# Stick-breaking heads scored in pairs with fp32 suffix products, and differential matrices combined before their transposition

## The chip, the cores and the metric

The kernel runs on one core of a Trainium2 chip as one program. The metric is the device time of one execution in microseconds (us). The engines are TensorE (PE, with its weight loads as PEld), VectorE (DVE), ScalarE (ACT), GpSimd (POOL) and SyncE (SP), which here issues the loads of the weights. They run side by side and meet through semaphores.

## What is computed

256 tokens of width 1024 pass through two layers of a first block and two layers of a second block, all in fp32. The first block (mLSTM, block-sparse and compressed attention, feed-forward) is not touched. A layer of the second block is:

```python
h = rms_norm(x, g_pre)
qa, ka, va, ga, qs, ks, vs, gs, qf, kf, vf, gf, ff = split(h @ w_in)   # 12 x 512 columns, and 8
ya = diff_attention(rope(qa), rope(ka), va, lam, lambda_init, subln) * silu(ga)
yb = stick_breaking_attention(qs, ks, vs) * silu(gs)
yc = forgetting_attention(qf, kf, vf, cumsum(log_sigmoid(ff + f_bias))) * silu(gf)
x = x + rms_norm(concat([ya, yb, yc]) @ w_out, g_post)
```

Differential attention has 4 heads of two softmax matrices each, over 64 features, and a value of width 128:

```python
p = softmax(where(allowed, s, -inf))        # for both matrices of a head
w = p[:, :, 0] - lam * p[:, :, 1]
o = w @ v                                   # then rms_norm(o, sub_gain) * (1 - lambda_init)
```

Stick-breaking attention has 8 heads of 64 features:

```python
log_keep = where(strict, log_sigmoid(-z), 0.0)
log_rest = cumsum(log_keep, reverse=True) - log_keep
a = where(strict, exp(log_sigmoid(z) + log_rest), 0.0)
o = a @ v
```

## The kernel before

**Units.** Nearly all work is the weight products. A unit is 512 KB of weights, 256 rows by 512 columns or 128 by 1024. SP loads it to one of four buffers `raw`; ACT copies it to `w_hi` in fp32r (L1193); DVE, for some units GpSimd, takes the remainder `w_lo` = `raw` - `w_hi` (L1561); PE then makes three products of parts, hi x hi, hi x lo and lo x hi (L754 to L756). ACT and DVE prepare the unit three ahead of the one at which PE stands (`AHEAD = 3`). A buffer of w_hi is free again when PE has finished the unit four before, which is what `released` waits for.

**Order.** Each layer has one list of steps, written out by hand; every engine walks through the same list in the same order and does its own part of each step. In the second block, `side2(p)` puts the attention steps behind unit p of the layer (12 projections of four units, p = 0 to 47, then the output units). `GROUPS`, `LAGS` or `V_LAG` and the numbers in `side2` say at which p a stage of a head stands. On each engine all steps wait in this order: an instruction that waits for a semaphore holds everything behind it on its engine.

**Differential heads**, 8 matrices h, from p = 12 on, one and a half units apart. S: scores of h and h+1 issued in turn, with the first on partitions 0 to 63 and the second on 64 to 127, to PSUM banks 4 and 5 (`score_pair`, L869); DVE adds the mask, takes the row maxima and writes to one of three buffers `probs` (L1639 to L1645). E: ACT's exponentials with their row sums (L1231, L1233). T: three transpositions on PE (L897) and ACT's copy to `probsT` (L1237). V: three products with the values (L904 to L906). After both matrices of a head, `epilogue_diff` on DVE takes the reciprocals of the row sums, scales the two results, adds them and sums their squares (L1959 to L1967). After the last one GpSimd applies norm, gain and gate (L1522 to L1530).

**Stick-breaking heads**, h = 0 to 7, from p = 26 on, one and a half units apart, with keys on the partitions. Z: two fp32 score products of 256 and 128 columns and two bf16 products that add the mask (L1120 to L1123), then on ACT abs, exp and log of 384 columns (L1422 to L1424) to `softp`, two buffers. K, one unit later: DVE adds max(z, 0) from PSUM (L2062) and splits the sum to `keep_hi` and `keep_lo` in fp32r (L2066, L2067). R, three units after Z: six fp32r products with the constant matrices `suffix` (L1130 to L1132) subtract the suffix sums from the scores, in the same PSUM bank; ACT's exp to `probs` (L1426). V, four units after Z: three products with the values (L1143 to L1145); `gated` multiplies by the gates.

**Forgetting heads** follow from p = 41 on with the same stages as the differential ones (S with two more products at L878).

Of the kernel before, what the change touches and what calls it, by code (L numbers as in the profile page):

```python
# [99 lines left out]
def hybrid_blocks(nc, x, w_in, b_if, conv_qk, m_norm, moba_qk_norm, nsa_q_norm, nsa_k_norm, cmp_pe,  # L100
# [78 lines left out]
    def head_steps(name, h, stage, groups_of):  # L179


        if stage == "S" and h % 2 == 0:
            for c in range(2):
                use((*name, "S", h + c), 4 + c)
        elif stage == "T":
            use((*name, "T", h), 6)
        elif stage == "V":
            g, r = divmod(h, groups_of)
            if r == 0:
                use((*name, "O", g), 7)  # L190
            if r == groups_of - 1:
                done((*name, "O", g))
        step(*name, stage, h)

    def stick_steps(l, h, stage):


        if stage == "Z":
            use(("stick", l, "Z", h), 4 + h % 3)
        elif stage == "R":  # L200
            use(("stick", l, "R", h), 4 + h % 3)
# [169 lines left out]
    for l in range(L):  # L371
# [75 lines left out]
    with ExitStack() as ctx:  # L447
# [52 lines left out]
        suffix = sb("suffix", [P, 2, P], F32R)  # L500
# [33 lines left out]
        row_sum, row_inv = few(2, 4, NT), few(4, NT)  # L534
        kc_s = few(4)
# [35 lines left out]
        keep_hi, keep_lo = exact("keep_hi", vecs_at, 0, 2, 384), exact("keep_lo", vecs_at, 768, 2, 384)  # L571
# [40 lines left out]
        diff_mixed = sem("diff_mixed")  # L612
        mix_ready = sem("mix_ready")
        u_hi_ready, u_ready = sem("u_hi_ready"), sem("u_ready")
        keep_ready = sem("keep_ready")
# [113 lines left out]
        def _(pe):  # L729
# [152 lines left out]

            def head_stage(kind, l, stage, h):
                name = (kind, l)
                if stage == "E":
# [6 lines left out]
                elif stage == "T":  # L892

                    pe.wait_ge(exp_ready, nth_head(kind, l, h))
# [4 lines left out]
                else:  # L899
                    g, r = divmod(h, GROUPS[kind])  # L900
                    drained(pe, (*name, "T", h))
# [5 lines left out]
                    if r == GROUPS[kind] - 1:  # L907
# [176 lines left out]
            for l in range(L):  # L1084
                for s in timeline[1][l]:
# [28 lines left out]
                    elif kind == "stick" and s[2] == "Z":  # L1114
                        h = s[3]
                        head_inputs(kind, l, "Z", h)
                        b = HD * (h % 2)
                        q, k = featT[b:b + HD, h // 2, :], featT[b:b + HD, 4 + h // 2, :]
                        ps = open_bank(("stick", l, "Z", h))
                        pe.matmul(ps[:, 0:T], k[:, 0:P], q, start=True, stop=False, skip_group_check=True)  # L1120
                        pe.matmul(ps[:, T:T + P], k[:, P:T], q[:, P:T], start=False, stop=False, skip_group_check=True)
                        pe.matmul(ps[:, 0:P], ident_b, strict_b, start=False, stop=False, skip_group_check=True)
                        close(pe.matmul(ps[:, T:T + P], ident_b, strict_b, start=False, stop=False, skip_group_check=True), s)  # L1123
# [44 lines left out]
        def _(act):  # L1168
# [201 lines left out]
            for l in range(L):  # L1370
                for s in timeline[1][l]:
# [744 lines left out]
```

## Time and profile before

| | |
|---|---|
| Median of 3 runs | 1177.3 us (1176.02 to 1179.41) |
| Profiled execution | 1181.94 us, span 1180.1 us, granted clock 0.974 |
| PE busy | 1131.2 us (96%) |
| PEld busy | 989.7 us (84%) |
| DVE busy | 741.5 us (63%) |
| ACT busy | 627.6 us (53%) |
| POOL busy | 111.7 us (9%) |
| Chain that ended last | PE 77%, DVE 13%, ACT 6%, issue 3% |

The span runs from the first to the last instruction; what is missing to the execution's own time lies around it. Layer 0 of the second block is at about 721 to 941 us of the span, layer 1 from there to the end. Busy time of PE counts pipelined products, whose printed durations overlap; the distance of two starts is what one takes. One fp32 product of the program stands as two records in the timeline.

### The profile page before, as it was taken

The page shows a single profiled execution, that of the slowest core. Times are in us where ns is not written, and L with a number is a line of the kernel's source. Part 1 is how long each engine was busy: PE and PEld are TensorE (multiplying, and loading weights), DVE is VectorE, ACT ScalarE, POOL GpSimd, SP SyncE. Part 2 cuts the span into 40 slices and gives each one's busy share as a digit, 9 for nine tenths or more (in the row PEclk, how much of TensorE's full clock was granted, in tenths as well). Part 3 has the DMA queues.
Part 4 walks back from the last instruction along what each step waited for, and adds up shares of the span by engine and source line. Part 5 has one row for each costly group of instructions (what it writes and reads, how often), then busy time and mean ns, then how long its engine had stood idle before and what let it go on. Part 6 is the DMA issues. An engine that isn't in the chain of part 4 may idle for free.

```text
span 1180.1 us, 17617 instructions
## 1 busy us (share of the span) xinstructions
PE 1131.2 (96%) x6888; PEld 989.7 (84%) x6888; DVE 741.5 (63%) x1275; ACT 627.6 (53%) x989; POOL 111.7 (9%) x99
## 2 busy tenths in 40 slices
PE   8899989999999899989999999999999989999997
PEld 6788779889988788769899887798988767989885
DVE  4786657555556876667555556667555566775555
ACT  4544655544545535746444545565657446656572
POOL 0324010000000324110000000003000000030000
PEclk8988999999999988999999999999999989999999
DMA  8625235555555425235555555444443445444431
GB/s 295 187 77 165 101 107 195 179 191 185 180 195 168 153 77 170 93 112 190 185 187 188 180 189 186 159 147 139 125 143 107 143 151 161 146 126 132 143 123 56
DMA packets 88959, 181.16 MB, mean 154 GB/s; under 512 B 8669, under 2 KB 19805, under 8 KB 88877
## 3 DMA queue, kind: packets, MB, share of 16 engines
q1 hardware_dynamic: 87437, 175.78, 45.9%
q10 hardware_dynamic: 1440, 4.26, 1.0%
q8 instruction: 55, 0.90, 0.3%
q14 instruction: 27, 0.22, 0.1%
HBM read 178.97 MB, written 1.05 MB: 153 GB/s over the span
## 4 chain that ended last, share of the span: by engine, by line
PE 77%; DVE 13%; ACT 6%; issue 3%; DMA 1%; POOL 1%; DVEq 0%; POOLq 0%; SPq 0%; ACTq 0%
PE bank L754 22%; PE bank L756 21%; PE bank L755 21%; DVE w_lo L1561 2%; PE bank L831 2%; ACT w_hi L1193 2%; PE bank L992 2%; PE bank L869 1%; PE bank L897 1%; DVE vecs L1570 1%; PE bank L1120 1%; DVE xn L1847 1%; PE bank L905 1%; PE bank L906 1%; PE bank L904 1%
## 5 line engine op out<-in xcount | busy, mean ns | idle before, releaser
L1561 DVE TENSOR_TENSOR w_lo<-raw,w_hi 128x1024 fp32r<-128x1024 f32 x296 | 366.3, 1241 | 297.6 <-ACT w_hi L1193 293.9
L1193 ACT ACTIVATE w_hi<-raw 128x1024 fp32r<-128x1024 f32 (+1 forms) x320 | 335.1, 1051 | 240.0 <-PE bank L756 205.7
L754 PE MATMUL bank<-h_hi,w_hi 128*128 128x256 f32 x896 | 262.7, 293 | 3.6 <-DVE w_lo L1561 2.1
L755 PE MATMUL bank<-h_lo,w_hi 128*128 128x256 f32 x896 | 257.5, 287 | 0.0
L756 PE MATMUL bank<-h_hi,w_lo 128*128 128x256 f32 x896 | 257.3, 287 | 0.0
L754 PE MATMUL bank<-w_hi,h_hi 128*128 128x512 f32 (+1 forms) x448 | 183.1, 409 | 5.8 <-DVE h_lo L1580 5.3
L754 PEld LDWEIGHTS bank<-h_hi,w_hi 128*128 128x128 f32 x896 | 176.1, 197 | 8.5 <-DVE w_lo L1561 3.4
L755 PEld LDWEIGHTS bank<-h_lo,w_hi 128*128 128x128 f32 x896 | 176.2, 197 | 0.5
L755 PE MATMUL bank<-w_lo,h_hi 128*128 128x512 f32 (+1 forms) x448 | 176.6, 394 | 0.0
L756 PE MATMUL bank<-w_hi,h_lo 128*128 128x512 f32 (+1 forms) x448 | 176.5, 394 | 0.0
L756 PEld LDWEIGHTS bank<-h_hi,w_lo 128*128 128x128 f32 x896 | 175.9, 196 | 0.0
L754 PEld LDWEIGHTS bank<-w_hi,h_hi 128*128 128x128 f32 x448 | 85.9, 192 | 23.9 <-DVE w_lo L1561 6.0
L754 PE MATMUL bank<-w_hi,u_hi 128*128 128x512 f32 x256 | 101.3, 396 | 0.0
L756 PEld LDWEIGHTS bank<-w_hi,h_lo 128*128 128x128 f32 x448 | 86.1, 192 | 17.8
L756 PE MATMUL bank<-w_hi,u_lo 128*128 128x512 f32 x256 | 101.0, 395 | 0.0
L755 PE MATMUL bank<-w_lo,u_hi 128*128 128x512 f32 x256 | 101.0, 394 | 0.0
L755 PEld LDWEIGHTS bank<-w_lo,h_hi 128*128 128x128 f32 x448 | 86.2, 192 | 14.8
L1455 POOL TENSOR_TENSOR w_lo<-raw,w_hi 128x1024 fp32r<-128x1024 f32 (+1 forms) x24 | 57.9, 2416 | 104.5 <-ACT w_hi L1193 104.4
L1237 ACT ACTIVATE probsT<-bank 128x384 f32<-128x384 f32 x56 | 27.4, 489 | 70.6 <-PE bank L897 70.1
L754 PE MATMUL bank<-w_hi,mixT_hi 128*128 128x512 f32 x128 | 54.1, 422 | 3.9 <-DVE mixT_lo L1580 3.9
L756 PEld LDWEIGHTS bank<-w_hi,u_lo 128*128 128x128 f32 x256 | 48.2, 188 | 11.3
L754 PEld LDWEIGHTS bank<-w_hi,u_hi 128*128 128x128 f32 x256 | 48.3, 189 | 10.4
(295 smaller groups left out, 1502.2 us busy)
## 6 DMA issues: line engine op xcount, KB each, us to landing
raw<-in_w_in SPq DMA_DIRECT2D x144, 512.0 KB, 3.8
raw<-in_w_ff SPq DMA_DIRECT2D x128, 512.0 KB, 4.0
raw<-in_w_out SPq DMA_DIRECT2D x40, 512.0 KB, 3.2
raw<-in_cmp_w SPq DMA_DIRECT2D x8, 512.0 KB, 4.5
raw<-in_w_in SPq DMA_DIRECT2D x8, 404.0 KB, 3.8
x_sb<-in_x SPq DMA_DIRECT2D x2, 512.0 KB, 7.4
gain<-in_norm_ffn ACTq DMA_DIRECT2D x2, 512.0 KB, 6.5
gain<-in_pre_norm ACTq DMA_DIRECT2D x2, 512.0 KB, 5.0
```

Of the source, the lines that this page charges most:

```text
L754: pe.matmul(out_ap, s_hi, m_hi, start=start, stop=False, **kw)
L755: pe.matmul(out_ap, s_hi, m_lo, start=False, stop=False, **kw)
L756: return pe.matmul(out_ap, s_lo, m_hi, start=False, stop=stop, **kw)
L831: mm = pe.transpose(ps[:, n * P:(n + 1) * P], src[:, i, k * P:(k + 1) * P], ident)
L869: mm = pe.matmul(ps[c][:, lo:lo + cols], q[:, i * P:(i + 1) * P], k[:, 0:cols], start=i == 0, stop=i == 1 and last == "scores", skip_group ...
L897: mm = pe.transpose(ps[:, b * P:(b + 1) * P], probs[:, h % 3, b * P:(b + 1) * P], ident)
L904: pe.matmul(ps[:, lo:lo + width], probsT[:, h % 3, 0:P], value(0), start=True, stop=True)
L992: mm = pe.matmul(ps[:, 16 * v:16 * v + NC_CMP], w[:, a, :], blocksT[:, v, 8 * half + a, :], start=(half == 0 and a == 0), stop=(half == 1 ...
L1193: act.activation(slot(w_hi, u), slot(raw, u), ACT.Copy).then_inc(hi_ready, 1)
L1237: free(act.activation(probsT[:, h % 3, :], ps[:, 0:384], ACT.Copy), (*name, "T", h))
L1455: pool.tensor_tensor(slot(w_lo, u), slot(raw, u), slot(w_hi, u).bitcast(F32), ALU.subtract)\
L1561: dve.tensor_tensor(slot(w_lo, u), slot(raw, u), slot(w_hi, u).bitcast(F32), ALU.subtract)\
```

## The change

- Differential heads: a new stage C between E and T. DVE computes `first + second * factor` for the exponentials of the two matrices of a head, with factor = -lam * (sum of first) / (sum of second) per row, in place in `first` (`combine_diff`). T and V run for even h only. `epilogue_diff` reads one result of 256 columns and multiplies it by the reciprocal of the first sum. T stands one unit later than before, and GpSimd's norm follows `V` of h = 6 at p = 25, before h = 7 at p = 26.
- Stick-breaking heads: Z of h and h+1 in one step every three units (`stick_pair`), products of the two heads in turn, to banks 4 and 5. K of both one unit later, R of both two units later, V of h three and of h+1 four units later. K keeps its first operation only; R makes three fp32 products from `softp` with the constants themselves. `keep_hi`, `keep_lo`, `suffix` and the semaphore `keep_ready` go.

```diff
         elif stage == "V" and name[0] == "diff":
+            use((*name, "O", h // 2), 7)
+            done((*name, "O", h // 2))
...
-        V_LAG = {"diff": 4, "fox": 3}
+        LAGS = {"diff": (("V", 4), ("T", 3), ("C", 2), ("E", 1), ("S", 0)), "fox": (("V", 3), ("T", 2), ("E", 1), ("S", 0))}
...
-                for stage, lag in (("V", V_LAG[name[0]]), ("T", 2), ("E", 1), ("S", 0)):
-                    for h in range(8):
+                for stage, lag in LAGS[name[0]]:
+                    for h in range(0, 8, 2 if name[0] == "diff" and stage in ("V", "T", "C") else 1):
...
-            for stage, lag in (("V", 4), ("R", 3), ("K", 1), ("Z", 0)):
+            for stage, lag in (("V", 3), ("R", 2), ("K", 1), ("Z", 0)):
                 for h in range(8):
-                    if int(26 + 1.5 * h) + lag == p:
+                    late = h % 2 if stage == "V" else 0
+                    if 26 + 3 * (h // 2) + lag + late == p:
                         stick_steps(l, h, stage)
...
+            def stick_pair(l, h):
...
+                for lo, i in ((0, 0), (T, 1)):
+                    for c in range(2):
+                        b = HD * c
+                        q, k = featT[b:b + HD, h // 2, i * P:T], featT[b:b + HD, 4 + h // 2, i * P:(i + 1) * P]
+                        pe.matmul(ps[c][:, lo:lo + T - i * P], k, q, start=i == 0, stop=False, skip_group_check=True)
+                for lo in (0, T):
+                    for c in range(2):
+                        mm = pe.matmul(ps[c][:, lo:lo + P], ident_b, strict_b, start=False, stop=False, skip_group_check=True)
+                        if lo:
+                            close(mm, keys[c])
...
-                    pe.wait_ge(exp_ready, nth_head(kind, l, h))
+                    if kind == "diff":
+                        pe.wait_ge(diff_weights, 4 * l + h // 2 + 1)
+                    else:
+                        pe.wait_ge(exp_ready, nth_head(kind, l, h))
...
-                        pe.wait_ge(keep_ready, 8 * l + h + 1)
                         ps = open_bank(("stick", l, "R", h))
-                        for kp in (keep_hi[:, h % 2, :], keep_lo[:, h % 2, :]):
-                            pe.matmul(ps[:, 0:T], suffix[:, 0, :], kp[:, 0:T], start=False, stop=False, skip_group_check=True)
-                            pe.matmul(ps[:, P:T], suffix[:, 1, :], kp[:, T:T + P], start=False, stop=False, skip_group_check=True)
-                            mm = pe.matmul(ps[:, T:T + P], suffix[:, 0, :], kp[:, T:T + P], start=False, stop=False,
-                                           skip_group_check=True)
-                        close(mm, s)
+                        keep = softp[:, h % 2, :]
+                        after, every = const[:, C_RTRI:C_RTRI + P], const[:, C_NONES:C_NONES + P]
+                        pe.matmul(ps[:, 0:T], after, keep[:, 0:T], start=False, stop=False, skip_group_check=True)
+                        pe.matmul(ps[:, T:T + P], after, keep[:, T:T + P], start=False, stop=False, skip_group_check=True)
+                        close(pe.matmul(ps[:, P:T], every, keep[:, T:T + P], start=False, stop=False, skip_group_check=True), s)
...
-                        if h >= 2:
-
-                            act.wait_ge(keep_ready, 8 * l + h - 1)
...
-                    elif s == ("diff", l, "V", 7):
+                    elif s == ("diff", l, "V", 6):
...
-                        link(dve.tensor_copy(suffix[:, 0, :], const[:, C_RTRI:C_RTRI + P]))
-                        link(dve.tensor_copy(suffix[:, 1, :], const[:, C_NONES:C_NONES + P]))
...
+                def combine_diff(g):
+
+                    first, second = probs[:, (2 * g) % 3, :], probs[:, (2 * g + 1) % 3, :]
+                    inv, factor = row_inv[:, 0:2, :], row_inv[:, 2, :]
+                    dve.wait_ge(exp_ready, nth_head("diff", l, 2 * g + 1))
+                    link(dve.reciprocal(inv, row_sum[:, g % 2, 0:2, :]))
+                    link(dve.scalar_tensor_tensor(factor, inv[:, 1, :], lam[:, 3:4], row_sum[:, g % 2, 0, :], ALU.mult, ALU.mult))
+                    link(dve.tensor_copy(first_inv[:, g % 2, :], inv[:, 0, :]))
+                    link(dve.scalar_tensor_tensor(first[:, 0:P], second[:, 0:P], factor[:, 0:1], first[:, 0:P], ALU.mult, ALU.add))
+                    dve.scalar_tensor_tensor(first[:, P:3 * P], second[:, P:3 * P], factor[:, 1:2], first[:, P:3 * P],
+                                             ALU.mult, ALU.add).then_inc(diff_weights, 1)
...
-                    ov = src(name)[:, :].rearrange("p (c i d) -> p c i d", c=2, i=NT)
-                    inv = row_inv[:, 0:2, :]
-                    link(dve.reciprocal(inv, row_sum[:, g % 2, 0:2, :]))
-                    link(dve.tensor_scalar(inv[:, 1, :], inv[:, 1, :], lam[:, 3:4], None, ALU.mult))
-                    t = o_tmp[:, :].rearrange("p (c i d) -> p c i d", c=2, i=NT)
-                    free(dve.tensor_tensor(t, ov, inv.unsqueeze(3).broadcast_to([P, 2, NT, P]), ALU.mult), name)
-                    tt(y_diff[:, :, g, :], t[:, 0], t[:, 1], ALU.add)
+                    ov = src(name)[:, 0:2 * P].rearrange("p (i d) -> p i d", i=NT)
+                    free(dve.tensor_tensor(y_diff[:, :, g, :], ov, first_inv[:, g % 2, :].unsqueeze(2).broadcast_to([P, NT, P]),
+                                           ALU.mult), name)
...
-                        if h >= 2:
-
-                            filled(dve, ("stick", l, "R", h - 2))
-                        link(dve.tensor_copy(keep_hi[:, h % 2, :], softp[:, h % 2, :]))
-                        dve.tensor_tensor(keep_lo[:, h % 2, :], softp[:, h % 2, :], keep_hi[:, h % 2, :].bitcast(F32),
-                                          ALU.subtract).then_inc(keep_ready, 1)
```

## Rows read from the trace of the kernel before

**Rows 1.** Stretches: bounds, busy us (instructions) per engine, granted clock, DMA share, GB/s.
```profile
820.00:860.00 40.00, 40.00 (x290) 37.03 (x288) 25.35 (x32) 25.42 (x39) 5.84 (x3) 1.00 0.39 125
```

**Rows 2.** Waits of PE, 740 to 926 us: total, times, longest.
```profile
PE bank L897 <- ACT probs L1233: 0.7, 1, 0.7
PE bank L754 <- DVE w_lo L1561: 0.3, 1, 0.3
```

**Rows 3.** Timeline of PE, V and T of differential heads: start us, duration, instruction.
```profile
778.27 0.38 PE L904 MATMUL bank<-arena,probsT 128*128 128x128 f32 x2
...
778.94 0.49 PE L897 MATMUL bank<-const,probs 128*128 128x128 f32 x3
779.18 0.36 PE L754 MATMUL bank<-h_hi,w_hi 128*128 128x256 f32 x1
779.39 0.28 PE L755 MATMUL bank<-h_lo,w_hi 128*128 128x256 f32 x1
779.50 0.28 PE L756 MATMUL bank<-h_hi,w_lo 128*128 128x256 f32 x1
```

**Rows 4.** Timeline of PE, the first two T of a layer.
```profile
767.40 0.49 PE L897 MATMUL bank<-const,probs 128*128 128x128 f32 x3
767.65 0.48 PE L754 MATMUL bank<-w_hi,h_hi 128*128 128x512 f32 x1
...
770.49 0.49 PE L897 MATMUL bank<-const,probs 128*128 128x128 f32 x3
```

**Rows 5.** Timeline of PE, last differential V and first stick scores.
```profile
811.83 0.39 PE L904 MATMUL bank<-arena,probsT 128*128 128x128 f32 x2
...
812.59 0.70 PE L1120 MATMUL bank<-arena 64*128 64x256 f32 x2
...
813.44 0.23 PE L1122 MATMUL bank<-masks 128*128 128x128 bf16 x1
...
813.54 0.48 PE L754 MATMUL bank<-w_hi,h_hi 128*128 128x512 f32 x1
```

**Rows 6.** Timeline of PE, the scores of a differential pair.
```profile
760.96 0.93 PE L869 MATMUL bank<-vecs 64*128 64x128 f32 x8
761.82 0.50 PE L754 MATMUL bank<-w_hi,h_hi 128*128 128x512 f32 x1
```

**Rows 7.** Timeline of PE, suffix products of the first and the last head.
```profile
822.93 0.28 PE L1130 MATMUL bank<-keep_hi,suffix 128*128 128x256 f32 x1
...
823.65 0.70 PE L1120 MATMUL bank<-arena 64*128 64x256 f32 x2
...
1099.08 0.36 PE L1130 MATMUL bank<-keep_hi,suffix 128*128 128x256 f32 x1
...
1099.79 0.44 PE L754 MATMUL bank<-w_hi,h_hi 128*128 128x512 f32 x1
```

**Rows 8.** Timeline of DVE behind the first stick scores.
```profile
816.35 1.22 DVE L1561 TENSOR_TENSOR w_lo<-raw,w_hi 128x1024 fp32r<-128x1024 f32 x1 [0.91 <-ACT w_hi L1193]
817.50 0.55 DVE L2062 SCALAR_TENSOR_TENSOR vecs<-bank,vecs 128x384 f32<-128x384 f32 x1
...
820.26 2.17 DVE L1561 TENSOR_TENSOR w_lo<-raw,w_hi 128x1024 fp32r<-128x1024 f32 x1
```

**Rows 9.** Timeline of DVE, a remainder ahead of the first T.
```profile
767.13 1.23 DVE L1561 TENSOR_TENSOR w_lo<-raw,w_hi 128x1024 fp32r<-128x1024 f32 x1 [1.17 <-ACT w_hi L1193]
```

**Rows 10.** Timeline of PE, fp32 products of full height in the first block.
```profile
504.00 0.65 PE L1040 MATMUL bank<-xn 128*128 128x256 f32 x2
504.49 0.39 PE L1041 MATMUL bank<-xn 128*128 128x128 f32 x2
```

**Rows 11.** Timeline of ACT behind the first stick scores.
```profile
813.76 0.49 ACT L1422 ACTIVATE vecs<-bank 128x384 f32<-128x384 f32 x1 [4.02 <-PE bank L1123]
...
815.28 1.04 ACT L1193 ACTIVATE w_hi<-raw 128x1024 fp32r<-128x1024 f32 x1
```

**Rows 12.** Timeline of GpSimd, two products of the differential norm.
```profile
820.05 3.53 POOL L1529 TENSOR_TENSOR xn<-xn,sub_gain 128x512 f32<-128x512 f32 x2
```

More of the change, by code:

```diff
@@ L186, in head_steps @@
             use((*name, "T", h), 6)
+        elif stage == "V" and name[0] == "diff":
+            use((*name, "O", h // 2), 7)
+            done((*name, "O", h // 2))
         elif stage == "V":
@@ L195, in stick_steps @@
     def stick_steps(l, h, stage):
-        if stage == "Z":
-            use(("stick", l, "Z", h), 4 + h % 3)
+        if stage == "Z" and h % 2 == 0:
+            for c in range(2):
+                use(("stick", l, "Z", h + c), 4 + c)
         elif stage == "R":
-            use(("stick", l, "R", h), 4 + h % 3)
+            use(("stick", l, "R", h), 4 + h % 2)
         elif stage == "V":
@@ L499, in hybrid_blocks @@
         rows = sb("rows", [8, 3, T])
-        suffix = sb("suffix", [P, 2, P], F32R)
         row_stack = sb("row_stack", [STACK, T], F32R)
@@ L534, in hybrid_blocks @@
         row_sum, row_inv = few(2, 4, NT), few(4, NT)
+        first_inv = few(2, NT)
         kc_s = few(4)
@@ L570, in hybrid_blocks @@
         softp = vecs[:, 3072 + 2048:3072 + 2048 + 768].rearrange("p (b t) -> p b t", b=2)
-        keep_hi, keep_lo = exact("keep_hi", vecs_at, 0, 2, 384), exact("keep_lo", vecs_at, 768, 2, 384)
         post_gain = vecs[:, 1536:1536 + D]
@@ L611, in hybrid_blocks @@
         h_ms_ready, h_rstd_ready = sem("h_ms_ready"), sem("h_rstd_ready")
-        diff_mixed = sem("diff_mixed")
+        diff_weights, diff_mixed = sem("diff_weights"), sem("diff_mixed")
         mix_ready = sem("mix_ready")
         u_hi_ready, u_ready = sem("u_hi_ready"), sem("u_ready")
-        keep_ready = sem("keep_ready")
         copied, sel_ready = sem("copied"), sem("sel_ready")
@@ L881, in score_pair @@
                                 close(mm, pair[c][0])
+            def stick_pair(l, h):
+                head_inputs("stick", l, "Z", h)
+                keys = [("stick", l, "Z", h + c) for c in range(2)]
+                ps = [open_bank(key) for key in keys]
+                for lo, i in ((0, 0), (T, 1)):
[4 more added lines that the diff above has]
+                for lo in (0, T):
+                    for c in range(2):
+                        mm = pe.matmul(ps[c][:, lo:lo + P], ident_b, strict_b, start=False, stop=False, skip_group_check=True)
+                        if lo:
+                            close(mm, keys[c])
             def head_stage(kind, l, stage, h):
                 name = (kind, l)
-                if stage == "E":
+                if stage in ("E", "C"):
                     return
@@ L900, in head_stage @@
                     g, r = divmod(h, GROUPS[kind])
+                    last = kind == "diff" or r == GROUPS[kind] - 1
                     drained(pe, (*name, "T", h))
@@ L906, in head_stage @@
                     mm = pe.matmul(ps[:, lo + width:lo + 2 * width], probsT[:, h % 3, 2 * P:3 * P], value(1), start=False, stop=True)
-                    if r == GROUPS[kind] - 1:
+                    if last:
                         close(mm, (*name, "O", g))
@@ L1114, in _ @@
                     elif kind == "stick" and s[2] == "Z":
[L1115 to L1123, printed above, removed]
+                        if s[3] % 2 == 0:
+                            stick_pair(l, s[3])
                     elif kind == "stick" and s[2] == "R":
                         h = s[3]
-                        pe.wait_ge(keep_ready, 8 * l + h + 1)
                         ps = open_bank(("stick", l, "R", h))
-                        for kp in (keep_hi[:, h % 2, :], keep_lo[:, h % 2, :]):
-                            pe.matmul(ps[:, 0:T], suffix[:, 0, :], kp[:, 0:T], start=False, stop=False, skip_group_check=True)
-                            pe.matmul(ps[:, P:T], suffix[:, 1, :], kp[:, T:T + P], start=False, stop=False, skip_group_check=True)
-                            mm = pe.matmul(ps[:, T:T + P], suffix[:, 0, :], kp[:, T:T + P], start=False, stop=False,
-                                           skip_group_check=True)
-                        close(mm, s)
+                        keep = softp[:, h % 2, :]
[3 more added lines that the diff above has]
+                        close(pe.matmul(ps[:, P:T], every, keep[:, T:T + P], start=False, stop=False, skip_group_check=True), s)
                     elif kind == "stick" and s[2] == "V":
@@ L2049, in _ @@
                             row_max((kind, l), s[3], C_CHUNK if kind == "diff" else C_CAUSAL)
+                        elif s[2] == "C":
+                            combine_diff(s[3] // 2)
+                        elif s[2] == "V" and kind == "diff":
+                            epilogue_diff(s[3] // 2)
                         elif s[2] == "V" and s[3] % GROUPS[kind] == GROUPS[kind] - 1:
                             g = s[3] // GROUPS[kind]
-                            if kind == "diff":
-                                epilogue_diff(g)
-                            else:
-                                gated(("fox", l, "O", g), 2, g, row_sum[:, g % 2])
+                            gated(("fox", l, "O", g), 2, g, row_sum[:, g % 2])
                     elif kind == "stick" and s[2] == "K":
```

## The prediction

> **What bounds the kernel now.** I first read the table of stretches. Between 820 and 860 us, in the part of the second block where the stick-breaking heads run, TensorE (PE) is busy 40.00 of 40 us at a granted clock of 1.00, while VectorE (DVE) and ScalarE (ACT) are busy 25.35 and 25.42 us [rows 1]. Next the list of waits, for PE alone over layer 0 of the second block: the largest entry is 0.7 us, and it belongs to the forgetting heads, which the change leaves alone [rows 2]. So PE is the bound, with no slack to give away, and the other engines only matter where a new wait makes PE stand still. Then the timeline of PE, where I take the distance from one start to the next, since the printed durations overlap. A half matmul of a weight product follows the last one by 0.11 to 0.12 us, but the first behind a head's step takes 0.21 us [rows 3]; each interruption of the weight stream thus costs about 0.09 us beside its own work. Last the timelines of ACT and DVE, for the chains that will feed PE.
>
> **Differential heads.** Before, every one of the 8 matrices of a layer has its own transposition (T) and product with V (V). Now DVE folds the second of a pair into the first, and T and V run for even h alone: four of each go per layer. A V and the T behind it run from 778.27 to 779.18, 0.67 + 0.24 = 0.91 us [rows 3]. In the places of a layer this gives: at step 14 a T alone, 0.25 us [rows 4]; at steps 17, 20 and 23 a V and a T, 3 x 0.91 = 2.73 us; at step 26 a V of 0.76 us [rows 5], of which I keep 0.09 us, since the scores behind it must still break into the stream. Sum 3.65 us. At steps 14, 17, 20 and 23 nothing is left between two units, which saves 4 x 0.09 = 0.36 us. That is 4.0 us per layer, **8.0 us** for both. ACT loses four copies per layer, which is off the path and worth nothing.
>
> What comes in is DVE's combination (step C): a reciprocal, two operations on two or four elements, and two scalar-tensor-tensors of 128 and 256 columns. No such operation from SBUF alone is in the trace; the nearest row is the 384-column one of the stick heads, 0.55 us [rows 8]. Five times that, 2.75 us, is the upper end; 0.55 us for all the columns together, with small ones at nothing, the lower. I take 1.5 us, because three of the five are tiny. The epilogue loses two operations of about the same work, so DVE's load stays; with 25 of 40 us it has room [rows 1]. Is T late? C(0) stands in DVE's queue behind the remainder (w_lo) of a unit that ends at 767.13 + 1.23 = 768.36 [rows 9]; plus 1.5 gives 769.9. T(0) now comes where T(1) was, 770.49 [rows 4], less the 0.34 us saved at step 14: 770.15. It fits by 0.3 us, so I price the wait at nothing. Behind C wait the next remainder, needed three units later, and the row maxima of the next pair. At the upper end of C, T would be late by 1.0 us, 8 us over the eight pairs.
>
> **Scores of the stick heads.** One head takes 0.85 us for its two fp32 products of 64 rows and 0.10 us for the two mask products: 812.59 to 813.54 [rows 5]. Sixteen are 15.2 us. The new step issues two heads in turn, on partitions 0 to 63 and 64 to 127. The scores of a differential pair are built so already: they hold the same 384 columns for each of two heads and take 0.86 us for both [rows 6], as much as one stick head alone. Add the masks, four instead of two: 0.10 to 0.35 us (what two take, and a whole stream of four as far apart as weight halves [rows 3]); I take 0.24. A pair costs 1.1 us, eight 8.8 us. Six of these now follow a V, where breaking in costs 0.09 us that an R step hid before: 0.5 us. Saving 15.2 - 9.3 = **5.9 us**. If the two heads did not overlap, it would be 2 x 0.95 = 1.9 us a pair and nothing saved.
>
> **Suffix sums.** Now six fp32r products per head, 0.72 us for the first [rows 7], 0.71 for the last; the sixteen read the same way lie between 0.62 and 0.81 and add up to 11.8 us. After: three fp32 products of 256, 128 and 128 columns. An fp32 product of 256 columns with full height takes 0.49 us including its entry [rows 10], so 0.40 without; one of 128 columns takes 0.67 / 3 = 0.22 us [rows 3]. That is 0.84 to 0.93; I take 0.88, 14.1 us in all: **+2.3 us**. Fewer instructions, then, but more PE time. A boundary less per layer in the stick part (-0.2 us for both).
>
> PE's own work thus changes by -8.0 - 5.9 + 2.3 - 0.2 = **-11.8 us**.
>
> **The new wait.** Before, R of a head came three units after its Z; now R of both heads comes two units after. In between lies: ACT's three operations per head, 815.28 - 813.76 = 1.52 us each [rows 11], for two heads; the next w_hi on ACT; its w_lo on DVE; and then the K of DVE. For one head K(0) began 817.50 and lasted 0.55, so it ended 4.51 us after the scores (813.54) [rows 5, 8]. With a second head on ACT ahead of the w_hi: 6.03 us. PE meanwhile has two units, 2 x 2.84 = 5.68 us (767.65 to 770.49 is one [rows 4]), and in the pairs 2 to 4 of a layer a V between them, 0.67 us more. So those three just fit, and the first pair of a layer waits 0.35 us. But GpSimd's norm of the differential heads runs beside it, 3.53 us for its two products [rows 12], and the w_lo that met it took 2.17 instead of 1.22 us [rows 8]. I expect it to meet this w_lo too: GpSimd starts one unit earlier, 4 us before what the row shows, but has further products behind these: +0.95 us on the chain. I take 1.2 us per layer, **+2.4 us**, with ends of 0 and 2.1 per layer. Behind the waiting R on PE stand the weight products; ACT and DVE run on meanwhile.
>
> How long DVE is held is where a rule of the Trainium skill weighs in (SBUF — State Buffer, section Who interferes with whom): a DVE instruction with two SBUF inputs and a GpSimd instruction reading SBUF exclude one another, and the second to start stands still until the first ends. The row agrees in kind, 2.17 us against 1.22. By the rule the K, with one input in PSUM, would not be held, but a w_lo that just missed could stand a whole GpSimd product; then the sum would come out about 1.8 us higher for both layers.
>
> The removed conversions of K (L2066, L2067) and of the suffix matrices (L1716, L1717) lie on DVE, which PE doesn't wait for here [rows 2]; I price them at nothing. No DMA is issued or moved.
>
> **Sum.** -11.8 + 2.4 = -9.4 us. The profiled execution took 1181.94 us (span 1180.1 and 1.8 around it), so 1172.5 of its kind. Its time lies 4.6 us above the median of 1177.3, which becomes 1167.9: **1168 us**.
>
> **Rivals.** (a) No stall: DVE's chain keeps up as it does now, and the whole 11.8 us shows, perhaps 1 more by cheaper masks: 1165. For it: only 0.35 us is missing without GpSimd. Against: the 2.17 us. (b) Slower: the chain of Z, ACT, w_hi, w_lo and K is late at every pair, because K falls behind one more remainder. A remainder comes once per unit, in step with the buffers that PE frees, so K would come one unit, 2.84 us [rows 4], after the time reckoned above: 3.2 us late at the first pair of a layer and 2.5 at the other three, 21.4 us in all, 1.9 more where GpSimd runs: 1177.3 - 11.8 + 23.3 = 1188.8. It decides from 11.8 / 8 = 1.5 us per pair on. For it: a margin of nearly nothing in three of four pairs, and a chain through four queued pieces of two engines. Against: the order of the queues, as the rows after 813.54 show it, has only one w_lo in front of K [rows 8]. (c) The two stick heads don't overlap, because their products begin with 256 columns and have masks behind: the 5.9 us go, 1173.8. Against: the differential pair of the same size takes 0.86 us. (d) The combination does not arrive in time for T at most pairs, 0.5 us each: 4 us back, 1172.
>
> **Chances.** Forecast as it stands 0.60; (a) 0.20; (c) 0.06; (d) 0.08; (b), or a half of it, 0.06. A change under 0.3%, 3.5 us, can't be told from none in this kernel. Forecast, (a), nearly all of (d) and half of (c) are faster: 0.91; same 0.05; slower 0.04. Range: down to (a) with the low ends of masks and R, 1163.5; up past the upper end of the two waits and (d), 1173.
>
> **What would show it.** Right: T and V of the differential heads half as many; a pair of stick scores about 1.1 us; R of two heads about 1.75 us in two equal parts; a gap on PE ahead of R of heads 0 and 1 in each layer, released by the K of DVE, and none ahead of the other R; GpSimd's products beside that w_lo. Wrong: gaps ahead of every R or T; two stick heads one behind the other; a granted clock below 1.00 in 740 to 920; an R over 1.0 us.

## The result, and the profile after

The changed kernel took 1162.56 us (median of 4 runs, 1160.23 to 1166.32) against 1177.47 (4 runs, 1176.02 to 1179.41): 14.9 us less. The ratio given with its 95% interval is 0.9864 (0.9839 to 0.9889), a little below the quotient of the two medians, 0.9873. The kernel is faster, and by more than the forecast 9.4 us: it ended 0.9 us below the range. Timed twice more, the same kernel gave ratios of 0.9928 and 0.9902 (below). All its 19 runs together have a mean of 1166.1 us (standard deviation 3.7), the 70 runs of the kernel before 1176.3 (3.0): 10.1 us less. The first timing was favourable to the change.

The page of the changed kernel, its span, busy time by engine, and the granted clock in 40 equal slices of the span, in tenths of full speed:

```profile
span 1159.3 us, 17421 instructions
...
PE 1109.0 (96%) x6816; PEld 967.6 (83%) x6816; DVE 722.1 (62%) x1257; ACT 622.8 (54%) x981; POOL 115.5 (10%) x99
...
PEclk9999999999999998999999999999999989999999
```

The profiled executions, 1181.94 and 1161.15 us, differ by 20.8. To see where, take two steps that the change doesn't touch: the last turned features before the second block, and the same of its layer 1. Timeline of PE, first before, then after:

```profile
721.53 0.66 PE L831 MATMUL bank<-const,xn 128*128 128x128 f32 x4 [0.47 <-DVE xn L1593]
...
941.30 0.66 PE L831 MATMUL bank<-const,xn 128*128 128x128 f32 x4 [1.09 <-DVE xn L1593]
```

```profile
711.20 0.66 PE L834 MATMUL bank<-const,xn 128*128 128x128 f32 x4 [0.48 <-DVE xn L1604]
...
926.01 0.66 PE L834 MATMUL bank<-const,xn 128*128 128x128 f32 x4 [1.10 <-DVE xn L1604]
```

Up to 721.53 and 711.20 both kernels run the first block, the same code but for two small casts: 10.3 us of the difference lie there. Layer 0 of the second block took 219.77 and 214.81, -5.0; layer 1 up to the last turned mix 216.17 and 210.65, -5.5; of this 0.2 lies in the piece ahead of the differential heads, which the change doesn't touch and which took 46.1 to 47.3 us in the profiles of either kernel. In what follows I cut the second block into stretches between such steps of PE. "Diff" runs from the turned features of the heads (756.39 us in the trace of before) to the first stick scores (812.59), "stick" from there to the first scores of the forgetting heads. All in us, each from one profile:

| kernel | block one | diff, layers 0 and 1 | stick, layers 0 and 1 |
|---|---|---|---|
| before | 721.53 | 56.20, 56.43 | 61.55, 61.55 |
| changed | 711.20 | 52.52, 52.39 | 60.30, 60.30 |

The rest of the second block, forgetting heads and output, is equal within 0.01 us in layer 0 (67.16 and 67.17).

**Differential heads after**, which answer to [rows 3]: V is followed by the weight stream, and the T behind it is gone.

```profile
764.14 0.38 PE L927 MATMUL bank<-arena,probsT 128*128 128x128 f32 x2
...
764.73 0.36 PE L757 MATMUL bank<-h_hi,w_hi 128*128 128x256 f32 x1
764.92 0.28 PE L758 MATMUL bank<-h_lo,w_hi 128*128 128x256 f32 x1
```

The new step C on DVE, behind the remainder that answers to [rows 9], and the T that waits for it, in the timelines of DVE and of PE:

```profile
757.10 1.23 DVE L1572 TENSOR_TENSOR w_lo<-raw,w_hi 128x1024 fp32r<-128x1024 f32 x1 [1.17 <-ACT w_hi L1207]
758.24 0.17 DVE L1968 RECIPROCAL small<-small 128x4 f32<-128x4 f32 x1
...
759.30 0.48 DVE L1972 SCALAR_TENSOR_TENSOR probs<-probs,small 128x256 f32<-128x256 f32 x1
```

```profile
759.84 0.55 PE L919 MATMUL bank<-const,probs 128*128 128x128 f32 x3
```

C takes 758.24 to 759.78, 1.54 us, and T starts 0.06 us after it. At this T and at the last one of each layer the margin was all used: there the weight load of T waits for C (three times in the second block, 1.1 us together, 0.4 at most). On PE little of it shows. The last T of layer 0 starts 0.37 us after the product ahead of it, where 0.23 is usual, and the next product 0.30 us after T for 0.25 before, so about 0.2 us is lost; at the other five T, C had ended 0.68 to 0.90 us before.

**Stick scores after** ([rows 5]): two heads in 0.85 us, four masks in 0.21 (a pair takes 1.06 us).

```profile
798.54 0.92 PE L895 MATMUL bank<-arena 64*128 64x256 f32 x8
799.39 0.40 PE L898 MATMUL bank<-masks 128*128 128x128 bf16 x4
799.60 0.48 PE L757 MATMUL bank<-w_hi,h_hi 128*128 128x512 f32 x1
```

**R of the first pair** ([rows 7]), with the one wait that is new; both heads take 1.78 us here, 1.67 to 1.78 elsewhere. Then DVE and GpSimd beside it ([rows 8, 12]), with the two GpSimd products of L1540 in rows of their own:

```profile
805.69 0.70 PE L1146 MATMUL bank<-vecs,const 128*128 128x256 f32 x2 [0.38 <-DVE vecs L2080]
806.23 0.38 PE L1147 MATMUL bank<-vecs,const 128*128 128x128 f32 x2
806.45 0.39 PE L1148 MATMUL bank<-vecs,const 128*128 128x128 f32 x2
806.67 0.60 PE L1146 MATMUL bank<-vecs,const 128*128 128x256 f32 x2
...
807.47 0.48 PE L757 MATMUL bank<-w_hi,h_hi 128*128 128x512 f32 x1
```

```profile
803.86 1.31 DVE L1572 TENSOR_TENSOR w_lo<-raw,w_hi 128x1024 fp32r<-128x1024 f32 x1 [5.27 <-ACT w_hi L1207]
805.09 1.14 DVE L2080 SCALAR_TENSOR_TENSOR vecs<-bank,vecs 128x384 f32<-128x384 f32 x2
806.31 1.22 DVE L1572 TENSOR_TENSOR w_lo<-raw,w_hi 128x1024 fp32r<-128x1024 f32 x1
```

```profile
802.79 1.30 POOL L1540 TENSOR_TENSOR xn<-xn,sub_gain 128x512 f32<-128x512 f32 x1
804.16 2.14 POOL L1540 TENSOR_TENSOR xn<-xn,sub_gain 128x512 f32<-128x512 f32 x1
806.38 3.42 POOL L1541 TENSOR_TENSOR mix<-xn,arena 128x1024 f32<-128x1024 f32 x1
```

The w_lo that should have been held took 1.31 us. It did meet GpSimd, but 0.23 us before the end of a product (802.79 + 1.30 = 804.09, where w_lo had started at 803.86). From then on GpSimd's products were the longer ones: the second of L1540 took 2.14 us for 1.30, and L1541, which began 0.07 us behind the next w_lo, took 3.42 us; in the trace of before the same product, L1530, took 2.39. The w_lo of before that took 2.17 us (820.26, [rows 8]) had started 0.21 us into such a product, the first of the two in [rows 12]:

```profile
820.05 1.30 POOL L1529 TENSOR_TENSOR xn<-xn,sub_gain 128x512 f32<-128x512 f32 x1
```

### The profile page after: what moved, and what is told of

Read it like the earlier page. It is cut to its first block, busy times and chain, and to the rows that moved or that the text cites. A ratio compares the mean times of both kernels' runs of the same rounds, so it can differ in the third digit from the quotient of the medians.

```text
span 1159.3 us, 17421 instructions
## 1 busy us (share of the span) xinstructions
PE 1109.0 (96%) x6816; PEld 967.6 (83%) x6816; DVE 722.1 (62%) x1257; ACT 622.8 (54%) x981; POOL 115.5 (10%) x99
## 4 chain that ended last, share of the span: by engine, by line
PE 75%; DVE 13%; ACT 6%; issue 3%; POOL 1%; DMA 1%; DVEq 0%; POOLq 0%; SPq 0%; ACTq 0%
PE bank L757 22%; PE bank L759 21%; PE bank L758 21%; DVE w_lo L1572 2%; ACT w_hi L1207 2%; PE bank L834 2%; PE bank L872 1%; PE bank L919 1%; DVE vecs L1581 1%; DVE xn L1856 1%; PE bank L1015 1%; PE bank L1146 1%; DMA raw<-in_w_in 1%; PE bank L929 1%; PE bank L928 1%
## 5 line engine op out<-in xcount | busy, mean ns | idle before, releaser
L757 PE MATMUL bank<-h_hi,w_hi 128*128 128x256 f32 x896 | 259.9, 290 | 4.5 <-DVE w_lo L1572 2.1
L757 PEld LDWEIGHTS bank<-h_hi,w_hi 128*128 128x128 f32 x896 | 173.6, 194 | 9.7 <-DVE w_lo L1572 3.1
L758 PEld LDWEIGHTS bank<-h_lo,w_hi 128*128 128x128 f32 x896 | 173.8, 194 | 0.5
L759 PEld LDWEIGHTS bank<-h_hi,w_lo 128*128 128x128 f32 x896 | 173.5, 194 | 0.0
L758 PEld LDWEIGHTS bank<-w_lo,h_hi 128*128 128x128 f32 x448 | 86.0, 192 | 14.9
L758 PEld LDWEIGHTS bank<-w_lo,u_hi 128*128 128x128 f32 x256 | 48.2, 188 | 10.4
```

Of the source, the lines that this page charges most:

```text
L757: pe.matmul(out_ap, s_hi, m_hi, start=start, stop=False, **kw)
L758: pe.matmul(out_ap, s_hi, m_lo, start=False, stop=False, **kw)
L759: return pe.matmul(out_ap, s_lo, m_hi, start=False, stop=stop, **kw)
```

## The experiments

**Is the first block part of the change?** The theory, A in what follows: the change is worth 10.5 us, all in the second block, and the rest of the 14.9 is the first block's own scatter. The rival, B: the change shortens the first block as well, since two casts are gone from it. First the kernel before, unchanged, once more.

> The unchanged kernel once more. The second block takes 219.8 us for layer 0 (from the first products of its first transpositions, 721.5, to those of layer 1, 941.3) and 216.2 us for layer 1 up to the last transpositions of the mix (1157.5). Theory A (the change is worth 10.5 us, all of it in the second block; the rest of the 14.9 us lies in the first block, whose time moves with the granted clock from execution to execution): the second block again takes 219.8 and 216.2 us within 0.5, and the first block, 721.5 us in the profile of before, comes out some us shorter this time, 712 to 721, with a higher mean clock than 0.974. Theory B (the first block of this kernel is always about 721 us, and the change shortened it): 720 to 722 again.

1177.27 us (12 runs, 1171.05 to 1181.48), ratio 0.9999 (0.9976 to 1.0021). Block one 719.04, diff 56.61 and 56.21, stick 61.55 and 61.54. The stretches of the second block repeat to a few tenths, the first block moved by 2.5 us. Layer 1 as a whole took 215.4 us, 0.8 less than in the first profile, where I had allowed 0.5; 0.6 of that lies in the piece ahead of the differential heads. Now the changed kernel, unchanged.

> The changed kernel once more. Theory A: the second block takes 214.8 and 210.7 us again, the first block anything between 711 and 721 us, and against the kernel before the ratio of medians lies at 1 - 10.5/1177 = 0.991, with chance excursions of some us. Theory B: first block 711 us again, ratio 0.986 to 0.988 as in the first timing.

1167.88 us (9 runs, 1161.64 to 1172.69), ratio 0.9928 (0.9901 to 0.9955). Block one took **721.65** us, as in the first profile of the kernel before; diff 52.64 and 52.41, stick 60.30 and 60.33. So the changed kernel has the long first block too: the rival falls. What differs is the granted clock. Over the five profiles of the two kernels (one of them is shown at the end of the experiments) the mean granted clock of the execution and the length of block one go together: 0.973 and 721.65 us, 0.974 and 721.53, 0.976 and 719.04, 0.983 and 715.91, 0.984 and 711.20. Table of stretches (bounds, length, busy us of PE, PEld, DVE, ACT, POOL, granted clock, DMA share, GB/s) of before, of the first profile of the changed kernel, and of this one:

```profile
80.00:90.00 10.00, 10.00 (x64) 10.00 (x64) 7.25 (x16) 2.66 (x5) 0.00 (x0) 0.67 0.51 150
...
440.00:450.00 10.00, 10.00 (x65) 9.50 (x64) 1.46 (x9) 4.15 (x5) 4.72 (x2) 0.70 0.46 155
```

```profile
80.00:90.00 10.00, 10.00 (x78) 10.00 (x77) 6.28 (x13) 3.66 (x6) 1.05 (x1) 0.83 0.68 205
...
440.00:450.00 10.00, 10.00 (x78) 9.17 (x77) 7.46 (x23) 5.81 (x15) 3.77 (x3) 1.00 0.61 211
```

```profile
80.00:90.00 10.00, 10.00 (x64) 10.00 (x64) 7.23 (x16) 2.61 (x5) 0.00 (x0) 0.67 0.51 149
...
440.00:450.00 10.00, 10.00 (x66) 9.50 (x65) 1.58 (x9) 4.15 (x5) 4.74 (x2) 0.71 0.46 153
```

**The differential part alone**, on the kernel before:

```diff
-                for stage, lag in (("V", V_LAG[name[0]]), ("T", 2), ("E", 1), ("S", 0)):
-                    for h in range(8):
+                for stage, lag in LAGS[name[0]]:
+                    for h in range(0, 8, 2 if name[0] == "diff" and stage in ("V", "T", "C") else 1):
+                def combine_diff(g):
...
```

> The kernel before with the differential part alone (combination, T and V for even h, epilogue, stages C at +2 and T at +3). By the traces of before and after: 3.7 us less in layer 0 between the turned features and the first stick scores, 4.0 us less in layer 1, nothing elsewhere: -7.7 us, 1169.8 from 1177.5. The prediction said -8.0. If the combination came too late for T it would show as a gap ahead of L919's counterpart; none is expected.

1169.51 us (6 runs), ratio 0.9938 (0.9917 to 0.9960), -7.3 us by the ratio. Diff 52.88 and 52.38, stick 61.56 and 61.56: -3.3 and -4.1. As expected.

**The stick part alone**, on the kernel before:

```diff
-            for stage, lag in (("V", 4), ("R", 3), ("K", 1), ("Z", 0)):
+            for stage, lag in (("V", 3), ("R", 2), ("K", 1), ("Z", 0)):
+            def stick_pair(l, h):
...
```

> The kernel before with the stick-breaking part alone. By the traces: -1.25 us per layer, -2.5 us, since pairing the scores saves 5.8 us, the fp32 products of R cost 2.2 and the waits ahead of R about 1. Under theory B, in which the two casts left out of the first block matter, it would be -7 us (2.5 and another 4.4).

1175.22 us (12 runs), ratio 1.0003 (0.9986 to 1.0021): nothing that can be measured. The stretches are 61.35 and 61.35, -0.2 us each instead of -1.25. The list of waits of PE (740 to 926 us) and the timelines of DVE and GpSimd of this kernel say why:

```profile
PE bank L1138 <- DVE vecs L2063: 1.4, 1, 1.4
```

```profile
811.39 2.33 DVE L1564 TENSOR_TENSOR w_lo<-raw,w_hi 128x1024 fp32r<-128x1024 f32 x1 [2.46 <-ACT w_hi L1199]
```

```profile
810.74 1.90 POOL L1526 TENSOR_TENSOR xn<-xn,small 128x1024 f32<-128x1024 f32 x1
```

Here the differential heads still end a unit later, the w_lo starts 1.25 us before the end of one of GpSimd's products (810.74 + 1.90), and it takes 2.33 us. The wait ahead of R, 1.4 us, is about what I had forecast for the whole change (1.2); in the changed kernel it is 0.38. The two parts are thus worth 1.0 us per layer more together than alone.

**The scores head by head**, in the changed kernel:

```diff
-                for lo, i in ((0, 0), (T, 1)):
-                    for c in range(2):
-                        b = HD * c
+                for c in range(2):
+                    b = HD * c
+                    for lo, i in ((0, 0), (T, 1)):
...
```

> The changed kernel, but the scores of the two stick heads are issued one head after the other, each with its masks, at the same place in the order. Theory A (the two heads overlap on PE because they are issued in turn on different halves of the rows): a pair goes from 1.06 to about 1.9 us, 3.4 us more per layer, less a wait ahead of the first R that shrinks by up to 0.38, so the stick stretch goes from 60.3 to about 63.3 us per layer, +6 us in all. Rival (the gain of the pair comes from being issued in one step, with fewer entries into the weight stream): 60.3 to 61 us.

1175.22 us (12 runs), ratio 0.9990 (0.9968 to 1.0011). Stick 63.17 and 63.17, +2.87 per layer. Timeline of PE:

```profile
809.54 0.92 PE L895 MATMUL bank<-arena 64*128 64x256 f32 x4
810.39 0.29 PE L897 MATMUL bank<-masks 128*128 128x128 bf16 x2
810.61 0.92 PE L895 MATMUL bank<-arena 64*128 64x256 f32 x4
```

Each head takes its 0.85 us again, and the pair with its masks 2.01 us (809.54 to 811.55) for 1.06. The stretch grows by less than four times that, since the waits ahead of R are gone. So the gain of the pair comes from issuing the products of the two heads in turn and not from one step for both. Whether the two heads must lie on different halves of the rows for it, no run here tests.

**The remainders back in R**, in the changed kernel, all else as it is:

```diff
-                        pe.matmul(ps[:, 0:T], after, keep[:, 0:T], start=False, stop=False, skip_group_check=True)
...
+                        pe.wait_ge(keep_ready, 8 * l + h + 1)
+                        for kp in (keep_hi[:, h % 2, :], keep_lo[:, h % 2, :]):
+                            pe.matmul(ps[:, 0:T], suffix[:, 0, :], kp[:, 0:T], start=False, stop=False, skip_group_check=True)
...
+                        link(dve.tensor_copy(keep_hi[:, h % 2, :], softp[:, h % 2, :]))
...
```

> The changed kernel with the split of K and the six fp32r products of R back, in the new order (R two units after Z). Theory A (R waits for the chain Z, ACT, w_hi, w_lo, K, which has no slack; PE saves 0.2 to 0.25 us per pair in R, but the two operations of 0.36 and 0.56 us stand behind K on DVE): about 1.3 us of wait at each pair and more at the first, where GpSimd runs: the stick stretch goes from 60.3 to 65 to 67 us per layer, +10 to +14 us in all. Rival (PE's own work decides): 59.4 us per layer, -1.8 us in all.

1189.92 us (6 runs), ratio 1.0111 (1.0080 to 1.0142). Stick 71.33 and 70.27, and the list of waits of PE, both layers:

```profile
PE bank L1149 <- DVE keep_lo L2091: 16.0, 14, 4.0
```

The direction of theory A, and worse than it said. R waits at 14 of the 16 heads, and the change loses all it gained and 13 us more. My rival (b) had such waits at every pair, but from another cause: it put K behind one more w_lo, and here K stands behind one w_lo as before. What makes R late is the cast and the subtraction themselves, and at the first pair GpSimd. DVE there, then the stretch behind the longest wait and two products of it on PE:

```profile
807.17 2.58 DVE L2091 TENSOR_TENSOR keep_lo<-vecs,keep_hi 128x384 fp32r<-128x384 f32 x1
```

```profile
810.00:820.00 10.00, 10.00 (x49) 8.64 (x50) 3.50 (x5) 3.40 (x6) 0.00 (x0) 0.74 0.34 105
```

```profile
813.20 0.63 PE L761 MATMUL bank<-w_lo,h_hi 128*128 128x512 f32 x1
813.63 0.63 PE L762 MATMUL bank<-w_hi,h_lo 128*128 128x512 f32 x1
```

Keep_lo takes 2.58 us there, beside a product of GpSimd that began 0.17 us ahead of it (L1546, 807.00, 2.34 us), and 0.56 at the second head. Both layers together lose 21.0 us against the changed kernel, and the waits are 16.0 us where that had 0.8. Part of the rest is the clock: behind the wait of 3.96 us the granted clock is 0.74 between 810 and 820 us, products of 512 columns follow each other at 0.43 us instead of 0.23, and the unit behind R takes 3.96 us against 2.83 in the changed kernel. So what the change got from dropping the remainders is not work of PE but this wait and the slower clock behind it.

**R three units after Z**, the changed kernel with other lags:

```diff
-            for stage, lag in (("V", 3), ("R", 2), ("K", 1), ("Z", 0)):
+            for stage, lag in (("V", 4), ("R", 3), ("K", 1), ("Z", 0)):
```

> The changed kernel with R three units after Z instead of two, and V one unit later too. Theory A (the only waits are the 0.38 us ahead of the first R of a layer and 0.3 us around the third pair, where U takes 3.18 instead of 2.95 us and R 1.77 instead of 1.67): both go, 60.3 becomes 59.7 us per layer, -1.2 us in all. Rival (another entry into the stream takes their place, as R then shares its place with Z): 60.3 us.

1169.87 us (12 runs), ratio 0.9954 (0.9928 to 0.9979), stick 61.89 and 61.89, +1.6 per layer: both theories missed. The waits ahead of R did go, but a new one came, at the scores of the next pair, which now stand right behind R and need the banks that ACT's exp has still to read. Three a layer; with the 0.6 us that were expected to go, 60.3 - 0.6 + 3 x 0.73 = 61.9:

```profile
PE bank L895 <- ACT probs L1437: 4.4, 6, 0.7
```

**Both edits together:**

> The two edits of the last two kernels together: the split of K and the fp32r products are back, and R comes three units after Z. Theory A: DVE has a unit more, so no wait, and the cheaper products count: 59.7 - 0.9 = 58.8 us per layer in the stick stretch, -3 us against the changed kernel. Rival (GpSimd holds the cast and the subtraction so long that R waits at the first pair all the same, as the 1.47 and 2.63 us of before suggest): 59.5 to 61 us.

1176.52 us (12 runs), ratio 1.0004 (0.9983 to 1.0025), stick 65.28 and 65.24. Missed again, for the same reason, with the waits of the rival on top, and with the clock: it is 0.75 between 820 and 830 us, behind the first of these waits, and 1.00 there in the changed kernel:

```profile
PE bank L898 <- ACT probs L1442: 4.4, 6, 0.7
PE bank L1149 <- DVE keep_lo L2091: 3.8, 4, 1.3
```

**K in the step of Z**, ahead of the next remainder in DVE's queue, R two units after Z as in the changed kernel:

```diff
-            for stage, lag in (("V", 3), ("R", 2), ("K", 1), ("Z", 0)):
+            for stage, lag in (("V", 3), ("R", 2), ("Z", 0), ("K", 0)):
```

> The changed kernel with K of both heads in the same step as Z, ahead of the next unit's remainder in DVE's queue; R stays two units after Z. Theory A (R waits only for a K that stands behind one w_lo): the 0.38 us ahead of the first R of a layer and the 0.3 us around the third pair go; DVE's w_lo starts no later than now, since its w_hi comes behind the same operations of ACT. Stick stretch 59.6 instead of 60.3 us per layer, -1.4 us in all. Rival (DVE, standing at K, delays a remainder that PE needs): 60.3 us or more, with waits of PE for w_lo.

1165.42 us (6 runs), ratio 0.9890 (0.9869 to 0.9911), stick 59.38 and 59.38, -0.92 per layer, a little more than the 0.7 expected. No wait ahead of R is left, and none for a remainder beyond the 0.6 us of both layers together that were there.

**The same with the remainders back:**

> As the last one, but with the split of K and the six fp32r products of R back. Theory A (what made these cost 10 us per layer two units after Z was only K's place behind w_lo): no wait from the second pair on, a wait of up to 1.5 us at the first, where GpSimd holds DVE's cast and subtraction; R saves 0.2 to 0.25 us per pair: 58.8 to 60.3 us per layer. Rival (the two operations themselves are too long for the chain): 62 us and more, with waits ahead of R at every pair.

1159.13 us (4 runs, 1156.12 to 1161.33), ratio 0.9834 (0.9814 to 0.9854): the fastest of all. Stick 58.17 and 58.17, 3.4 us per layer less than before the change and 2.1 less than with it, and less than the 58.8 at best that was expected. The ratio says 19.5 us, the stretches 14.5 (10.2 and twice 2.1); the rest is scatter of the kind seen in the first timing, and the profile has a first block of 710.95 us. Both heads' R in the timeline, first and last product and the next unit, and what is left of the wait:

```profile
817.33 0.28 PE L1149 MATMUL bank<-keep_hi,suffix 128*128 128x256 f32 x1
817.44 0.22 PE L1150 MATMUL bank<-keep_hi,suffix 128*128 128x128 f32 x1
817.50 0.28 PE L1151 MATMUL bank<-keep_hi,suffix 128*128 128x128 f32 x1
...
818.52 0.27 PE L1151 MATMUL bank<-keep_lo,suffix 128*128 128x128 f32 x1
```

```profile
PE bank L1149 <- DVE keep_lo L2091: 0.4, 2, 0.2
```

Two heads of six fp32r products take 1.3 us from the second pair on, where three fp32 products each take 1.67. So once K stands early the fp32 products of the change are a loss, 1.2 us per layer (59.38 against 58.17). Between this kernel and the one with K late lie 13.2 and 12.1 us in the two layers, the slower clock included, for one place in one queue.

**The changed kernel a third time**, beside these two:

> The changed kernel a third time, since the first timing gave 14.9 us and the second 8.6. Theory A: the second block again 10.2 to 10.5 us shorter than before, the first block anywhere between 711 and 722 us, and the ratio of medians near 0.991. Theory B (the change shortens the first block too): ratio below 0.989.

1166.63 us (6 runs), ratio 0.9902 (0.9883 to 0.9922). Block one 715.91, diff 52.37 and 52.39, stick 60.30 and 60.30. The interval of this timing holds 10.2 us (0.9913), as does that of the second; that of the first does not. All profiles of the two kernels, first and repeated, give the two stretches of the second block together some 10 us less in the changed kernel. And the three kernels above that have the two casts of the first block back took 711.97, 718.54 and 710.95 us there, so that these casts don't set its length. Theory A stands.

## Why the prediction was right and wrong

**What failed: the last step, from the profiled execution to the median and its range.** I took 9.4 us off the whole time and built the range from the unknown costs of the change alone; the scatter of what the change leaves alone I put at nothing. Of the 5.5 us that the forecast missed, 0.8 are in the second block, which did what was forecast within 1 us; the other 4.7 no experiment ties to the change. The time of a run also holds the first block, which took 711.20, 715.91 and 721.65 us in three profiles of the same changed kernel and 721.53 and 719.04 in two of the kernel before. Single runs of the kernel before differ by up to 14 us in one timing (1168.13 to 1182.39), its medians in the four timings run from 1174.38 to 1178.39, and a median of four has an error of some 2 (an estimate from the 3.0 and 3.7 us of single runs). A range down to 1163.5 left no room for that; the three runs that I had, 1176.02 to 1179.41, hid it. I had called 3.5 us the least change that can be told; two medians of the same kernel lie 4.0 apart. That the first timing fell on the side of the change was chance. That the profiled execution of before was itself a long one, 4.6 us over its median at a clock of 0.974, was in front of me, and I treated it as a constant.

**Differential heads: right.** Forecast 4.0 us per layer, measured 3.7 to 4.2 over the profiles with both kernels' stretches (56.20 to 56.61 against 52.37 to 52.64). C took 1.54 us for 1.5. The first T of layer 0 came 0.06 us behind C, where I had 0.3 us of margin, and three of the eight T wait for it by 0.1 to 0.2 us; rival (d), 0.5 us at most pairs, did not happen.

**Scores: right.** 1.06 us a pair for 1.1, with four masks in 0.21 us for 0.24. The head-by-head kernel shows that issuing in turn is the whole gain; rival (c) is out.

**Suffix sums: right.** 1.67 to 1.78 us per pair for 1.76, more PE time than the six fp32r products had. The forecast of the price was right; what the change bought with it, a chain without the two operations, I had priced at nothing, since I asked only what DVE's time was worth and not where K stood. The kernel with the remainders back shows its worth under this order: 10 to 11 us per layer, the slower clock included. I had taken each edit against the kernel before; this one is only worth something under the order that the change brings, with R two units after Z and K behind a w_lo.

**The wait ahead of R: place right, size wrong.** Forecast 0.35 us without GpSimd and 1.2 with it, at the first pair of a layer alone. Measured is a gap of 0.38 us. Against the kernel with K early, which has no such wait, the two units ahead and R take 6.09 + 1.78 us for 5.55 + 1.67, so the late K costs 0.65 us there. The third pair, for which I saw nothing, loses another 0.3 us: the unit ahead of R took 3.18 instead of 2.95 us, and R 1.78 instead of 1.67. There an operation of DVE that I had not counted stands between the w_lo and K, the gating of the first four heads (L1997, 830.10, 0.68 us). In all 1.8 us for both layers (twice 0.92) where I had 2.4. The chain was reckoned well. The term that was mis-sized is the 0.95 us for GpSimd: I took the delay of one w_lo from the row of before, but the delay depends on how much of GpSimd's product is left, and here it was 0.23 us. The rule of the Trainium skill (SBUF — State Buffer, Who interferes with whom) would hold such a w_lo until GpSimd's instruction ends. The traces agree as far as GpSimd's rough spans go: 2.17 us with 1.09 us of the product left, 2.33 with 1.25 left in the kernel with the stick part alone, 1.31 with 0.23 left, for 1.22 us undisturbed, each time held 0.14 us shorter than what was left.

Sum by the stretches: -7.7 (forecast -8.0) for the differential heads, -2.5 (forecast -3.8 + 2.4 = -1.4) for the stick heads, -10.2 in all against -9.4. Without the waits ahead of R, by the kernel with K early, PE's own work in the stick stretch fell by 4.3 us where I had 3.8, as R took 1.67 us a pair for 1.76 and the scores 1.06 for 1.1.

**Not settled:** why one execution gets the low clock in the first block longer than another. The rows show where it happens, and that it happens with either kernel; no run here tells what picks the execution.

## What to carry to other kernels

Where PE never rests, the start-to-start distances of the steps in the old trace give the price of a change of its work within some tenths per layer; the worth of an edit on a side engine is not its busy time but whether it stands in a chain that PE waits for, and moving one short step ahead of a long one in its queue can be worth more than leaving work out (K early with the remainders: 1159 us, K late with them: 1190). A long wait of PE can cost more than its length, since the granted clock behind it was lower (0.74 behind 3.96 us). Before stating a range, ask how far the untouched part moves from run to run; the second profile of the same kernel tells it. And before accepting a difference near that scatter, compare stretches between fixed steps instead of whole times.

## What the runs showed of the hardware

The granted clock of PE falls in the first block while PE is counted as busy throughout: 10.00 of 10 us at a clock of 0.67, that is, by two levels of 1.0 and 0.5, about two thirds of the time at the lower one of 1.2 GHz. In the trace of before PE was working there on products of 15 columns, and 256-column halves behind them follow each other at 0.21 us instead of 0.12:

```profile
85.81 4.17 PE L992 MATMUL bank<-blocksT,raw 128*128 128x15 f32 x26
...
91.14 0.41 PE L756 MATMUL bank<-h_hi,w_lo 128*128 128x256 f32 x1
91.35 0.41 PE L754 MATMUL bank<-h_hi,w_hi 128*128 128x256 f32 x1
...
94.59 0.28 PE L755 MATMUL bank<-h_lo,w_hi 128*128 128x256 f32 x1
94.71 0.28 PE L756 MATMUL bank<-h_hi,w_lo 128*128 128x256 f32 x1
```

In R an fp32r product of 128 columns is followed by the next at 0.06 us (817.44 to 817.50, K early with the remainders), one in full fp32 at 0.22 (806.23 to 806.45, changed kernel).
